# Two loops of the first stage put in turn, one subtraction moved to VectorE, and the merge's gate loads moved to POOL's queue

## What is computed

```python
mod = silu(c) @ w_ada + b_ada                    # w_ada 1024 x 6144: 24 blocks of 256 columns
sh1, sc1, ga1, sh2, sc2, ga2 = split(mod, 6)
h = rms(x, norm1_g) * (1.0 + sc1) + sh1          # prompt and sample rows
z = h @ w_in                                     # queries, keys, values, gates
...                                              # two attention branches, y_a and y_b
g_a, g_b = split(sigmoid(merge_l), 2)
x = x + ga1 * ((g_a * y_a + g_b * y_b) @ w_out)
...                                              # SwiGLU FFN
```

## Time and profile before

| | us |
|---|---|
| median of 3 runs (2085.28 to 2087.86) | 2087.17 |
| the profiled execution | 2087.93 |
| its span, first to last instruction | 2086.2 |
| TensorE busy in the span | 1968.0 (94%) |
| VectorE busy | 1163.8 (56%) |
| ScalarE busy | 678.8 (33%) |
| POOL busy | 151.2 (7%) |

### The profile page before, as it was taken

One profiled execution on the slowest core, in us unless ns is written; L12 is line 12 of the kernel. 1 busy time (PEld: TensorE's weight loads), 2 busy tenths in 40 slices (PEclk: granted clock), 3 DMA queues, 4 the chain that ended last, 5 costly groups with the idle time before them and its releaser, 6 DMA issues. The chain is left out here.

```text
span 2086.2 us, 34801 instructions
## 1 busy us (share of the span) xinstructions
PE 1968.0 (94%) x13032; PEld 1854.3 (89%) x13032; DVE 1163.8 (56%) x2531; ACT 678.8 (33%) x1273; POOL 151.2 (7%) x190
## 2 busy tenths in 40 slices
PE   5889999999996899999999999999999999999997
PEld 3658798789996788898898999999999999999997
DVE  5944333334244677777775556655656555555555
ACT  5623244331223566666573133311111010101011
POOL 1442100101300000000200000000000000000000
PEclk9999999999998899999899999999999999999999
DMA  9876553522001000000003531121212121211102
GB/s 312 272 210 192 157 175 107 149 92 64 28 25 66 1 1 1 1 1 1 1 1 102 185 123 58 51 61 30 60 30 60 30 60 30 60 40 51 40 0 82
DMA packets 151758, 157.10 MB, mean 75 GB/s; under 512 B 15859, under 2 KB 132483, under 8 KB 151604
## 3 DMA queue, kind: packets, MB, share of 16 engines
q1 hardware_dynamic: 140076, 130.73, 20.5%
q0 software_dynamic: 4656, 16.40, 2.3%
q10 hardware_dynamic: 6912, 8.46, 1.1%
HBM read 139.33 MB, written 18.32 MB: 76 GB/s over the span
## 5 line engine op out<-in xcount | busy, mean ns | idle before, releaser
L1877 DVE SCALAR_TENSOR_TENSOR l_x2T<-tail_bank,g_modT,l_x2T 128x344 f32<-128x344 f32 (+1 forms) x528 | 265.3, 565 | 102.5 <-PE tail_bank L1616 102.2
L1616 PE MATMUL tail_bank<-l_wo 128*128 128x344 f32 x1584 | 270.2, 319 | 2.8 <-DVE late_total_s L1883 2.8
L1616 PEld LDWEIGHTS tail_bank<-l_wo 128*128 128x128 f32 x1584 | 252.7, 188 | 3.3 <-issue 3.3
L1448 ACT ACTIVATE l_act<-tail_bank 128x344 f32<-128x344 f32 x66 | 30.2, 458 | 523.6 <-PE tail_bank L1598 523.5
L884 PE MATMUL nsa_out<-zs_z,nsa_probT 128*128 128x64 f32 (+1 forms) x1344 | 175.9, 276 | 5.2 <-DVE zs_z L1040 5.0
L884 PEld LDWEIGHTS nsa_out<-zs_z,nsa_probT 128*128 128x128 f32 x1344 | 168.7, 198 | 7.1 <-DVE zs_z L1040 6.9
L1598 PE MATMUL tail_bank<-late_words_hi,l_uhi 128*128 128x344 f32 x528 | 169.7, 321 | 3.3 <-DVE late_words_lo L1780 3.3
L1598 PE MATMUL tail_bank<-late_words_lo,l_uhi 128*128 128x344 f32 x528 | 169.3, 321 | 0.0
L1598 PE MATMUL tail_bank<-late_words_hi,l_ulo 128*128 128x344 f32 x528 | 169.2, 320 | 0.0
L1598 PE MATMUL tail_bank<-late_words_lo,late_wo 128*128 128x344 f32 x528 | 169.1, 320 | 0.0
L1598 PE MATMUL tail_bank<-late_words_hi,l_wo 128*128 128x344 f32 x528 | 169.1, 320 | 0.0
(11 more groups left out here) (500 smaller groups left out, 4319.1 us busy)
## 6 DMA issues: line engine op xcount, KB each, us to landing
mod_wr<-in_w_ada SPq DMA_DIRECT2D x24, 1024.0 KB, 5.6
kin_kin<-in_cache_kv SPq DMA_DIRECT2D x64, 256.0 KB, 3.5
late_gate<-in_w_ffn_in SPq DMA_DIRECT2D x22, 512.0 KB, 5.8
l_raw_o<-in_w_ffn_out SPq DMA_DIRECT2D x22, 512.0 KB, 3.7
late_raw<-in_w_ffn_in SPq DMA_DIRECT2D x22, 512.0 KB, 5.1
gate_d<-dec_gate ACTq DMA_DIRECT2D x48, 172.0 KB, 2.9
late_gate<-gate_d SPq DMA_DIRECT2D x8, 1032.0 KB, 5.4
dec_vin<-in_cache_kv SPq DMA_DIRECT2D x64, 128.0 KB, 2.2
```

What stands on the lines that cost most here:

```text
L1448: act.activation(sg[(j + c) % 2], pg[(j + c) % 2][:, 0:TCH], ACT.Silu).then_inc(silu_done, 1)
L1616: mm = pe.matmul(po[u % 4][:, 0:TCH], w[j][:, k * P:(k + 1) * P], a[j][:, tok(c)], start=(q == 0), stop=(q == 2))
L1877: mm = dve.scalar_tensor_tensor(out=here, in0=po[u % 4][:, 0:part_w(c)], scalar=g.modT[:, 5 * KD + k, NDEC:NC9], in1=here, op0=ALU.mult, o ...
```

## The change

There are three parts. One: a list `SEQUENCE` gives the order of loads and of work on all engines: weight blocks 0 to 11, then weight block 12 and piece 0, block 13 and piece 1 and so on to block 19 and piece 7, then blocks 20 to 23. Raw buffers and PSUM buffers go by the place `p` in it, the split buffers by the number of the weight block; the semaphores of the two kinds become one pair, `pm_full` and `pm_read`. `UNIT0` is 12 for 11. Two: the subtraction for the low half of `h` moves from POOL to VectorE, right behind the cast of the high half. Three: in the merge the gates are loaded from POOL's queue by a loop of its own, ahead of the loads of x, whose wait for the second merged block is gone; their semaphores aren't among those that are cleared.

The diff, without lines of context, 8 columns further left:

```diff
@@ -102,7 +102,9 @@
-    RATE, UNIT0 = 8, 11
+    RATE, UNIT0 = 8, 12
+    SEQUENCE = [("w", m) for m in range(12)] + [x for i in range(NZ) for x in (("w", 12 + i), ("z", i))] + [("w", m) for m in range(12 + NZ, NMOD)]
+    place = {x: p for p, x in enumerate(SEQUENCE)}
@@ -129,9 +131,8 @@
-w_hi, w_lo, mod_ps, mod_sb, modT_ps, modT_sb = (
-    s.sem(n) for n in ("w_hi", "w_lo", "mod_ps", "mod_sb", "modT_ps", "modT_sb"))
-z_ps, z_sb = s.sem("z_ps"), s.sem("z_sb")
+w_hi, w_lo, pm_full, pm_read, modT_ps, modT_sb = (
+    s.sem(n) for n in ("w_hi", "w_lo", "pm_full", "pm_read", "modT_ps", "modT_sb"))
@@ -150,18 +151,17 @@
-        for m in range(NMOD + NZ):
-            if m >= RAWS:
-                old = m - RAWS
-                if old < NMOD:
-                    sp.wait_ge(w_lo, old + 1)
+        for p, (kind, n) in enumerate(SEQUENCE):
+            if p >= RAWS:
+                old, k = SEQUENCE[p - RAWS]
+                if old == "w":
+                    sp.wait_ge(w_lo, k + 1)
...
-                    sp.wait_ge(z_ps, old - NMOD + 1)
-            if m < NMOD:
-                sp.dma_start(wr[m % RAWS][:], w_ada[:, :, m * WC:(m + 1) * WC]).then_inc(w_in[m % RAWS], 16)
+                    sp.wait_ge(pm_full, p - RAWS + 1)
+            if kind == "w":
+                sp.dma_start(wr[p % RAWS][:], w_ada[:, :, n * WC:(n + 1) * WC]).then_inc(w_in[p % RAWS], 16)
...
-                c = (m - NMOD) * ZC
-                sp.dma_start(wr[m % RAWS][:, :, 0:ZC], w_all[:, :, c:c + ZC]).then_inc(w_in[m % RAWS], 16)
+                sp.dma_start(wr[p % RAWS][:, :, 0:ZC], w_all[:, :, n * ZC:(n + 1) * ZC]).then_inc(w_in[p % RAWS], 16)
@@ -176,15 +176,6 @@
-
-        def low_h(u):
-            half, k = half_of(u), k_of(u)
-            cols = slice(half * 512, half * 512 + 512)
-            pool.wait_ge(h_hi, u + 1)
-            pool.tensor_tensor(g.hT_lo[:, k, cols], hf[:, u % 3, :], f32(g.hT_hi[:, k, cols]), ALU.subtract).then_inc(h_lo, 1)
-
-        for u in range(2 * KD):
-            low_h(u)
@@ -210,21 +201,20 @@
-        for m in range(NMOD):
-            loaded(act, m)
-            if m >= SPLITS:
-                act.wait_ge(mod_ps, m - SPLITS + 1)
-            act.activation(whi[m % SPLITS][:], wr[m % RAWS][:], ACT.Copy).then_inc(w_hi, 1)
-            if 1 <= m <= TT + 1:
-                if m > 1:
-                    act.wait_ge(sq_done, m - 1)
-                square(m - 1)
-            if m == TT + 1:
+        for p, (kind, n) in enumerate(SEQUENCE):
+            if kind == "w":
+                loaded(act, p)
+                if n >= SPLITS:
+                    act.wait_ge(pm_full, place["w", n - SPLITS] + 1)
+                act.activation(whi[n % SPLITS][:], wr[p % RAWS][:], ACT.Copy).then_inc(w_hi, 1)
+            if 1 <= p <= TT + 1:
+                if p > 1:
+                    act.wait_ge(sq_done, p - 1)
+                square(p - 1)
+            if p == TT + 1:
...
-            shifted(unit_at(m, 2))
-        for m in range(NMOD, NMOD + NZ):
-            shifted(unit_at(m, 2))
+            shifted(unit_at(p, 2))
@@ -241,7 +231,7 @@
-            pe.wait_ge(mod_sb, m + 1)
+            pe.wait_ge(pm_read, place["w", m] + 1)
@@ -258,35 +248,29 @@
-        for m in range(NMOD):
-            pe.wait_ge(w_lo, m + 1)
-            if m >= 3:
-                pe.wait_ge(mod_sb, m - 2)
-            for k in range(KD):
-                for q, b in enumerate((whi, wlo)):
-                    mm = pe.matmul(pm[m % 3][:], c18[:, k, :], b[m % SPLITS][:, k, :], start=(k == 0 and q == 0), stop=(k == KD - 1 and q == 1))
-            mm.then_inc(mod_ps, 1)
-            if m:
-                mod_transposed(m - 1)
-            if m == UNIT0:
+        for p, (kind, n) in enumerate(SEQUENCE):
+            if p >= 3:
+                pe.wait_ge(pm_read, p - 2)
+            if kind == "w":
+                pe.wait_ge(w_lo, n + 1)
+                for k in range(KD):
+                    for q, b in enumerate((whi, wlo)):
+                        mm = pe.matmul(pm[p % 3][:], c18[:, k, :], b[n % SPLITS][:, k, :], start=(k == 0 and q == 0), stop=(k == KD - 1 and q == 1))
+            else:
+                loaded(pe, p)
+                pe.wait_ge(coef, 3)
+                for k in range(KD):
+                    mm = pe.matmul(pm[p % 3][0:NDEC, 0:ZC], hs[:, k, :], wr[p % RAWS][:, k, 0:ZC], start=(k == 0), stop=(k == KD - 1))
+            mm.then_inc(pm_full, 1)
+            if p and SEQUENCE[p - 1][0] == "w":
+                mod_transposed(SEQUENCE[p - 1][1])
+            if p == UNIT0 - 1:
...
-            turned(unit_at(m))
+            turned(unit_at(p))
...
-        pe.wait_ge(coef, 3)
-        for i in range(NZ):
-            m = NMOD + i
-            loaded(pe, m)
-            if i < 3:
-                pe.wait_ge(mod_sb, min(NMOD, NMOD + i - 2))
-            else:
-                pe.wait_ge(z_sb, i - 2)
-            for k in range(KD):
-                mm = pe.matmul(pm[m % 3][0:NDEC, 0:ZC], hs[:, k, :], wr[m % RAWS][:, k, 0:ZC], start=(k == 0), stop=(k == KD - 1))
-            mm.then_inc(z_ps, 1)
-            turned(unit_at(m))
@@ -302,11 +286,15 @@
-        def mod_copied(m):
-            dve.wait_ge(mod_ps, m + 1)
-            if m >= 2:
-                dve.wait_ge(modT_ps, m - 1)
-            dve.tensor_copy(mod[m % 2][:], pm[m % 3][:]).then_inc(mod_sb, 1)
+        def read(p):
+            kind, n = SEQUENCE[p]
+            dve.wait_ge(pm_full, p + 1)
+            if kind == "w":
+                if n >= 2:
+                    dve.wait_ge(modT_ps, n - 1)
+                dve.tensor_copy(mod[n % 2][:], pm[p % 3][:]).then_inc(pm_read, 1)
+            else:
+                dve.tensor_copy(g.zd[:, n * ZC:(n + 1) * ZC], pm[p % 3][0:NDEC, 0:ZC]).then_inc(pm_read, 1)
@@ -320,7 +308,10 @@
-                dve.tensor_copy(g.hT_hi[:, k, half * 512:half * 512 + 512], hf[:, u % 3, :]).then_inc(h_hi, 1)
+                cols = slice(half * 512, half * 512 + 512)
+                dve.tensor_copy(g.hT_hi[:, k, cols], hf[:, u % 3, :]).then_inc(h_hi, 1)
+                dve.wait_ge(h_hi, u + 1)
+                dve.tensor_tensor(g.hT_lo[:, k, cols], hf[:, u % 3, :], f32(g.hT_hi[:, k, cols]), ALU.subtract).then_inc(h_lo, 1)
@@ -333,14 +324,15 @@
-        for m in range(NMOD):
-            dve.wait_ge(w_hi, m + 1)
-            dve.tensor_tensor(wlo[m % SPLITS][:], wr[m % RAWS][:], f32(whi[m % SPLITS][:]), ALU.subtract).then_inc(w_lo, 1)
-            if m >= 1:
-                mod_copied(m - 1)
-            if m >= 2:
-                mod_biased(m - 2)
-            if m == RATE + 1:
+        for p, (kind, n) in enumerate(SEQUENCE):
+            if kind == "w":
+                dve.wait_ge(w_hi, n + 1)
+                dve.tensor_tensor(wlo[n % SPLITS][:], wr[p % RAWS][:], f32(whi[n % SPLITS][:]), ALU.subtract).then_inc(w_lo, 1)
+            if p >= 1:
+                read(p - 1)
+            if p >= 2 and SEQUENCE[p - 2][0] == "w":
+                mod_biased(SEQUENCE[p - 2][1])
+            if p == RATE + 1:
@@ -350,19 +342,15 @@
-            if RATE + 1 <= m <= RATE + 4:
-                for t in range(2 * (m - RATE - 1), 2 * (m - RATE)):
+            if RATE + 1 <= p <= RATE + 4:
+                for t in range(2 * (p - RATE - 1), 2 * (p - RATE)):
...
-            high_h(unit_at(m, 3))
-            if m == UNIT0 + 1:
+            high_h(unit_at(p, 3))
+            if p == UNIT0:
...
-        mod_copied(NMOD - 1)
+        read(len(SEQUENCE) - 1)
...
-        for i in range(NZ):
-            dve.wait_ge(z_ps, i + 1)
-            dve.tensor_copy(g.zd[:, i * ZC:(i + 1) * ZC], pm[(NMOD + i) % 3][0:NDEC, 0:ZC]).then_inc(z_sb, 1)
-            high_h(unit_at(NMOD + i, 3))
@@ -1249,7 +1237,7 @@
-w_in, gate_in = [s.sem(f"w_in{i}") for i in range(2)], [s.sem(f"gate_in{i}") for i in range(2)]
+w_in, gate_in = [s.sem(f"w_in{i}") for i in range(2)], [s.pool_sem(f"tail_gate_in{i}") for i in range(2)]
@@ -1306,8 +1294,6 @@
-                sp.wait_ge(gate_free, n + 1)
-                sp.dma_start(gate[j], gate_v[ds(n * P, P), :, :]).then_inc(gate_in[j], 16)
@@ -1333,7 +1319,11 @@
-        pool.wait_ge(m_split, 2)
+        with pool.Fori(0, KD // 2) as i:
+            for j in range(2):
+                n = i * 2 + j
+                pool.wait_ge(gate_free, n + 1)
+                pool.dma_start(gate[j], gate_v[ds(n * P, P), :, :]).then_inc(gate_in[j], 16)
```

## The result

The changed kernel takes 2102.03 us in the median of 5 runs (2094.10 to 2107.64), the kernel before beside it 2087.17 (5 runs, 2085.28 to 2088.31): 1.0058 times as long, 95% interval 1.0040 to 1.0076. On another chip later it was 2097.39 against 2091.58, 1.0034 (1.0017 to 1.0051). It is slower, by 0.2 to 0.8%, and at 2102 or 2097 it lies beyond the 2095 of my range.

The account below looks back on a forecast made before the run. TensorE was taken as the bound almost everywhere, leaving the first stage and branch merge to respond: 2087.93 + 2.5 (seam) - 0.6 (merge gates) = 2089.8 us, 2089.1 for a median; own range 2087.5 to 2091.3, overall range 2084.5 to 2095.

Parts of the forecast that it names:

- The loop of a piece's buffer: First stage: a weight block reuses a piece's raw buffer, so piece i+2 ends 15.7 us after piece i, gap some 1.6.
- ScalarE was to set the seam: End of first stage: ScalarE starts 4.5 us later, its chain ends at 150.0, and VectorE waits for it: +2.5 us.
- The seam's pass-through: After the first stage: +2.5 us, plus one us for each us the stage ends beyond 144.9.
- Part 1: First stage: low halves move from POOL to VectorE; a unit costs VectorE 1.1 us after, 1.18 before: nothing lost.
- Part 3: Branch merge: gate loads move from SP's to POOL's queue; gain -0.6 us (0 to -0.9).
- the 0.6 us wait: Branch merge: TensorE's only wait for ScalarE, 0.6 us, expected to go when gate loads leave SP's queue.
- rival A: Alternating stretch: gaps let the clock fall to 1.2 GHz, up to 3 us a spell; two spells give 2095; chance 0.20.
- the new gaps of 1.6 us: Alternating stretch: TensorE waits some 1.6 us every second pair, near 82, 97, 113 and 129 us; forecast at full clock.
- the wait of 1.84: Kernel before, at 43.54 us: TensorE had stood for 1.84 us and kept the full clock.
- that of 2.99: Kernel before: TensorE waited 2.99 us until 58.66; within 60 to 61 us its clock was 0.50, still at 65.
- by that rule each of the gaps would bring a slow spell: Alternating stretch: skill's rule that bursts parted by load waits can start at half clock, read as against the change.

Follow-up runs that it names:

- filled: The changed kernel with twelve extra 18x144 matmuls ahead of TensorE's wait for each of weight blocks 13 to 19; 2092.15 us, 1.0014 of the kernel before.
- low_only: The kernel before with only the low-half subtractions of h moved from POOL to VectorE; 2090.89 us, 1.0016 of the kernel before.
- order_only: The kernel before with only SEQUENCE, weights and pieces in turn; low halves on POOL, gates on SP; 2096.21 us, 1.0039 of the kernel before.
- gates_only: The kernel before with only the merge's gate loads moved to POOL's queue; 2089.44 us, 0.9998 of the kernel before.
- after_again: The changed kernel run once more on another chip, with a second profile; 2097.39 us, 1.0034 of the kernel before.
- two_splits: The changed kernel with three raw buffers and two pairs of split buffers instead of three; 2101.90 us, 1.0063 of the kernel before.
- four_raw: The changed kernel with four raw buffers and two pairs of split buffers instead of three and three; 2088.00 us, 1.0003 of the kernel before.

## Why the prediction was wrong

**The forecast's mechanism held.** The loop of a piece's buffer was to take 15.7 us for two pairs with a gap of 1.6; it took 15.5 with 1.72. Piece 0 was to end at 73.9 and the stage at 144.9, with the queries at 162.15: filled, in which the clock holds, has 74.0, 145.4 and 162.4. ScalarE was to set the seam, and VectorE waits for its exponential in the row at 155.39. The seam's pass-through held too: +2.5 and the 5.3 us by which the stage's end, 150.2, lies beyond 144.9 would put the queries at 167.45; they start at 167.55.

**Part 1** held: VectorE's unit takes 0.41 + 0.69 = 1.1 us, and low_only and order_only show nothing lost. **Part 3** held: the 0.6 us wait is gone, 0.8 us by the stretch in gates_only, and the gates land in 5.4 to 8.8 us. In the changed kernel the stretch from the merge's first transposes to the first up-projection gives 1.1 (7.8 to 6.7); 0.5 of it is the first wait (1.9, before 2.4), which gates_only doesn't have, so it isn't of this part. Its cause wasn't tested.

**The step that failed is the choice between forecast and rival A**, that is, the sentence that the new gaps of 1.6 us lie nearer to the wait of 1.84 that went by without a spell than to that of 2.99. It put the price of the clock at nothing in the forecast, and gave A 0.20, on the strength of one row. In the five traces of this order with three buffers, 18 of 20 gaps of 1.6 to 2.2 us had a spell behind them; the first gap of the changed kernel's own trace, 1.72 us, is one of the two exceptions, and gaps of 1.62 and 1.71 had one, so within this range the length doesn't decide it. The size of the gap was also a little off: two pairs of 6.9 us in a loop of 15.7 leave 1.9 us, not 1.6. The Trainium skill's page TensorE: Matmul & The Clock Gate (HAM oscillation — how this bites in real kernels) tells of a kernel whose bursts of matmuls, parted by waits for loads, start at the lower clock each time. Its waits are two to three times as long as the gaps here, so "by that rule each of the gaps would bring a slow spell" went beyond what it states; what it describes is nevertheless what these five traces show.

**A's sizes were off too, and its number came near by luck.** I priced a spell at 3 us of stage and allowed two. Those at 102 and 119 us cost the loop 1.7 and 1.8 us (rounds of 17.2 and 17.1, in filled 15.5 and 15.3); in order_only three of them, in rounds of 17.0, cost 1.6 each. Another 1.6 us comes from the spell at 64 to 71 us, by which piece 0 ends late (75.6, in filled 74.0). It isn't A's: it began ahead of the pairs, and the kernel before has one at 60 to 66 us. Together that is the 5.1 us by which piece 6 ends later than in filled (125.4, 120.3); from there to the stage's end both take 25 us. Of the spell at 136 to 139 us nothing is seen, filled has one there too. So the profiled execution, 2094.1, meets A's 2095 with fewer us for each spell and one spell that A didn't have. The rest was in nobody's sum: the first five executions of the changed kernel lost 72 us of clock on average where the profiled one lost 63, and after_again lost 68.6 where before lost 63.7, which at the slopes above is 2 to 6 us. The range ended at 2095, where A's single value stood, and had no room above it.

**Still open** is where the longer runs lose their clock. Profiles stand for single executions. One of two_splits, with a span of 2105.4, shows it in stretches that no edit touches:

```profile
700.00:1150.00 450.00, 412.51 (x3005) 383.70 (x3005) 320.23 (x925) 279.31 (x703) 34.26 (x34) 0.94 0.03 11
```

The changed kernel's profile has 0.96 there. Whether the new order brings these spells about, or they merely fall as they fall, no run here tells. The same holds for most of what four_raw gained before 160 us and didn't keep.

## What to carry to other kernels

When a loop's period rests on a load, work out the gap that it leaves on TensorE, and ask whether the kernel ran without such gaps before: here regular gaps of 1.6 to 2.2 us in a stretch that had kept the full clock cost the stage 3.5 to 5 us, more than the loop itself (2.5 us). Before two kinds of work are put in turn, look at which kind's buffer each load takes over: with three buffers nearly every block of the pairs was loaded behind a piece's end, with four none was, and that decided between queries that start 8 us later and 6 us sooner. And where one execution differs from the next through the clock, compare spans and granted clocks of many runs, as a single profile can be the shortest of its kind.

## What the runs showed of the hardware

- Filling idle time with matmuls whose result is thrown away made a kernel faster by 0.2% (1.0034 to 1.0014), with nothing else changed: with 84 matmuls of 18x144, 0.24 us each by the profile, in the waits the clock stayed at 1.00 from 63 to 137 us.
- A filler isn't free where the clock falls while it runs: 14 matmuls of 128x344, of which the last ran at 0.50, took 3.17 us, 0.23 each, while 26 at the full clock took 4.27, 0.16 each.
- Gaps of TensorE of 1.6 to 2.2 us, 16 to 18 us apart, were followed by a clock of 0.50 in 18 of 20 cases, in five traces; seven gaps of 0.55 to 0.65 us and one of 1.32 in 43 us of the kernel before were not.
- A VectorE subtraction of 128x512 into fp32r took 0.69 us where the cast of the same size took 0.41, and the split of 128x2048 took 2289 ns in the changed kernel, where POOL has no subtractions, against 2363.
